# The expert gather of a two-model program: 12 row buffers for U in three quads, 12 for V in three rotating sets, V groups up to five behind U groups, and head queries one chunk earlier

## What is computed

```python
def peer_ffn(xm, w_query, sub_keys, expert_u, expert_v):      # per layer
    q = (xblk @ w_query).reshape(B, 128, 8, 2, 256)            # 8 heads, 512 wide
    s = einsum('bthpd,hpnd->bthpn', q, sub_keys)               # 2 x 128 key scores a head
    vals, idx = lax.top_k(s, 16)
    cand = vals[..., 0, :, None] + vals[..., 1, None, :]       # 256 candidates
    top_s, pos = lax.top_k(cand, 16)
    eidx = take_along_axis(cand_idx, pos)                      # 16 of 16384 experts
    g = softmax(top_s)
    h = einsum('btd,bthkd->bthk', xblk, expert_u[eidx])        # 16 dot products
    act = gelu(h) * g
    return einsum('bthk,bthkd->btd', act, expert_v[eidx])      # sum of 16 rows
```

## Time and profile before

| | |
|---|---|
| median of 3 runs | 3297.96 us (3285.51 to 3304.04) |
| profiled execution, span from first to last instruction | 3263.7 us, 34.3 us less than the median |
| instructions | 34887 |
| gather of layer 0 / layer 1 | about 240 to 1018 us / 1225 to 2005 us |
| busy: PE, DVE, ACT, POOL | 75%, 64%, 29%, 32% of the span |
| DMA | 886.31 MB; 536.94 MB of them by POOL's indirect DMAs |

### The profile page before, as it was taken

The page is one execution under the profiler, slowest core; times in us unless marked ns, Lnnn a source line. Parts: engine busy times, 40 slices in busy tenths (PEclk is TensorE's granted clock), DMA queues, the critical chain, the costliest instruction groups (busy, mean ns, idle before and its releaser), DMA issues.

```text
span 3263.7 us, 34887 instructions
## 1 busy us (share of the span) xinstructions
PE 2431.9 (75%) x12607; PEld 1727.6 (53%) x12607; DVE 2088.5 (64%) x4416; ACT 933.8 (29%) x1486; POOL 1043.1 (32%) x1060
## 2 busy tenths in 40 slices
PE   5996555544546997555545545999999999999998
PEld 4754422221103764422221102789879988997797
DVE  7878576666656958576666654655555555556654
ACT  3511011110112421011101112544554446445543
POOL 0105566666663105566566663100010001000000
PEclk9998777766667998677666766989999999999999
DMA  9858999999999839999999998345534542554353
GB/s 363 299 209 332 353 374 380 378 379 365 361 378 341 295 139 342 350 370 394 377 359 372 356 365 307 131 143 191 180 130 155 180 168 82 190 194 155 110 193 123
DMA packets 308642, 886.31 MB, mean 272 GB/s; under 512 B 22824, under 2 KB 32144, under 8 KB 308240
## 3 DMA queue, kind: packets, MB, share of 16 engines
q0 software_dynamic: 147456, 536.94, 42.9%
q1 hardware_dynamic: 161040, 347.51, 29.9%
HBM read 883.32 MB, written 1.05 MB: 271 GB/s over the span
## 4 chain that ended last, share of the span: by engine, by line
PE 46%; issue 31%; DVE 9%; another core or an unknown queue 6%; DMA 4%; SPq 2%; ACT 2%; POOL 1%; DVEq 0%; ACTq 0%; POOLq 0%
PE lin L837 7%; PE lin L838 7%; PE lin L839 7%; PE psT L839 2%; PE psT L838 2%; PE psS L838 2%; PE psS L839 2%; PE psT L837 2%; PE psS L837 2%; PE lin L1141 2%; PE psS L1097 2%; PE psS L887 2%; DMA ring<-in_w_in 2%; PE lin L1014 1%
## 5 line engine op out<-in xcount | busy, mean ns | idle before, releaser
L2454 DVE CUSTOM_DVE_ANT_0 proj<-proj,psT 128x1024 f32<-128x1024 f32 x512 | 606.1, 1218 | 211.1 <-DMA proj<-in_expert_u,eidx 120.5
L1928 DVE TENSOR_TENSOR weights_split<-ring,weights_split 128x1024 fp32r<-128x1024 f32 (+1 forms) x360 | 431.5, 1207 | 376.2 <-ACT weights_split L1712 373.6
L2787 POOL DMA_INDIRECT proj<-in_expert_u,eidx x512 | 481.5, 940 | 424.7 <-DVEq L2430 212.7
L1712 ACT ACTIVATE weights_split<-ring 128x1024 fp32r<-128x1024 f32 (+1 forms) x376 | 391.5, 1046 | 467.7 <-PE lin L839 291.6
L1141 PE MATMUL lin<-vbuf,rowb 128*32 128x512 f32 x1024 | 252.0, 879 | 266.8 <-issue 180.4
L2823 POOL TENSOR_TENSOR weights_split<-ring,weights_split 128x1024 fp32r<-128x1024 f32 x16 | 37.9, 2376 | 995.3 <-ACT weights_split L1712 995.3
L1141 PE MATMUL lin<-ring,rowb 128*32 128x512 f32 x896 | 208.8, 755 | 153.1 <-issue 107.1
L837 PE MATMUL lin<-weights_split,xT_high 128*128 128x512 f32 (+1 forms) x736 | 295.0, 401 | 19.6 <-issue 8.2
L839 PE MATMUL lin<-weights_split,xT_high 128*128 128x512 f32 (+1 forms) x736 | 288.1, 391 | 0.0
L2800 POOL DMA_INDIRECT ring<-in_expert_v,pT x224 | 211.0, 942 | 231.4 <-remote 86.8
L2800 POOL DMA_INDIRECT vbuf<-in_expert_v,pT x256 | 241.2, 942 | 115.5 <-issue 76.5
(11 more groups left out here) (336 smaller groups left out, 4943.9 us busy)
## 6 DMA issues: line engine op xcount, KB each, us to landing
ring<-in_mlp_w_up SPq DMA_DIRECT2D x32, 2048.0 KB, 8.1
ring<-in_mlp_w_down SPq DMA_DIRECT2D x32, 2048.0 KB, 7.9
ring<-in_w_in SPq DMA_DIRECT2D x14, 2048.0 KB, 14.1
ring<-in_w_query SPq DMA_DIRECT2D x14, 2048.0 KB
vbuf<-in_ada_w SPq DMA_DIRECT2D x12, 2048.0 KB, 12.9
ring<-in_diff_w_in SPq DMA_DIRECT2D x11, 2048.0 KB, 8.1
proj<-in_ada_w SPq DMA_DIRECT2D x24, 512.0 KB, 5.1
ring<-in_moba_w_in SPq DMA_DIRECT2D x6, 2048.0 KB, 8.0
```

Source lines behind the costliest of these rows:

```text
L1712: act.activation(part(p, 0, kind, w), raw_piece(slot, p, kind, w), ACT.Copy).then_inc(hi_ready, 1)
L1928: dve.tensor_tensor(part(p, 1, kind, w), raw_piece(slot, p, kind, w), part(p, 0, kind, w).bitcast(F32), ALU.subtract).then_inc(lo_ready, 1)
L2454: dve.tensor_tensor_reduce(ubuf[:, n % GB, :], ubuf[:, n % GB, :], x_row, 1.0, 0.0, ALU.mult, ALU.add, hdot[:, cb, k:k + 1]).then_inc(h_re ...
L2787: pool.indirect_dma_start(out=ubuf[:, (16 * c + k) % GB, :], out_offset=None, in_=table["u"], in_offset=bass.IndirectOffsetOnAxis(ap=eidx[ ...
```

## The change

U gets twelve rows in three quads: the old eight and `ring3`. `UQUAD` gives each group its quad: 0, 1, 0, 1 for the first four, then 2, 0, 1 in turn; a group waits for the dots of the last group that used its quad. Quad 2 is granted by `u_free` at the place of the second credit of L1249. V keeps three sets of buffers, used in rotation by the running number of the group and not by the set within the chunk; the last V group of a layer (63) goes to the quad of U group 61. The first credits of `v_free` are three in place of four, so V group 2 waits for the credit of L1258 and V group 3 for the sum of set 0. `LAGS` puts V groups behind U groups by 2, 2, 3, 4 in chunks 0 to 3, by 5 in chunks 4 to 13, and by 4 and 3 in the last two. `indices_by_pair(c + 2)` moves ahead of all sets of chunk c. Heads 4 to 7 are asked in chunks 3, 5, 7, 9 in place of 4, 6, 8, 10, with half the query behind the second set and half, with the key scores, behind the third (chunks 1 and 2: behind the first and the second, as before), and the keys' transposes no longer ahead of the chunk's sets. DVE's waits on `v_free` are renumbered to mean the same sums.

```diff
@@ -50,9 +50,13 @@
 NSET = 4
 SETROWS = TOPK // NSET
-VLAG = 2
-LANDED = 16 * PH * NT * TOPK // GB
-VLANDED = 16 * SETROWS * PH * NT
+NVB = 3
+GROUPS = 4 * PH * NT
+UQUAD = [0, 1, 0, 1] + [(2, 0, 1)[i % 3] for i in range(GROUPS - 4)]
+UBEFORE = [max([j for j in range(i) if UQUAD[j] == UQUAD[i]], default=None) for i in range(GROUPS)]
+UTIMES = [UQUAD[:i + 1].count(UQUAD[i]) for i in range(GROUPS)]
+VBUF = [q % NVB for q in range(GROUPS - 1)] + [NVB]
+VTIMES = [VBUF.count(b) for b in range(NVB + 1)]
 DEPTH2 = 4
@@ -204,7 +208,8 @@
 NCH = len(CHUNKS)
 ROWS_TAKEN = [1 + sum(CHUNKS[i][1] != CHUNKS[i - 1][1] for i in range(1, c + 1)) for c in range(NCH)]
-ASKED = {1: 2, 2: 3, 4: 4, 6: 5, 8: 6, 10: 7}
+ASKED = {1: 2, 2: 3, 3: 4, 5: 5, 7: 6, 9: 7}
+LAGS = [2, 2, 3, 4] + [5] * (NCH - 6) + [4, 3]
 SUM_AT = {u: q for q, u in enumerate(SUMS)}
@@ -346,15 +351,21 @@
             return {8: psS[:, 1, :], 0: psT[:, 0, :], 2: psT[:, 1, :], 4: lin[:, 2, :], 6: lin[:, 3, :]}[b]
 
-        def vrow(i):
-
-            if i < 4:
-                return vbuf[:, i, :]
-            if i < 8:
-                return ring3[:, (i - 4) * D:(i - 3) * D]
-            if i < 12:
-                return ring2[:, (i - 8) * D:(i - 7) * D] if i < 11 else pr1
-            return vbuf[:, i - 8, :]
+        def urow(i, b):
+
+            if UQUAD[i] == 2:
+                return ring3[:, b * D:(b + 1) * D]
+            return ubuf[:, 4 * UQUAD[i] + b, :]
+
+        def vrow(q, b):
+
+            if VBUF[q] == NVB:
+                return urow(GROUPS - 3, b)
+            if VBUF[q] == 0:
+                return vbuf[:, b, :]
+            if VBUF[q] == 1:
+                return ring2[:, b * D:(b + 1) * D] if b < 3 else pr1
+            return vbuf[:, 4 + b, :]
 
@@ -486,8 +497,8 @@
         ps_used = sem("peer_scores_copied")
         idx_ready = sem("expert_indices_ready")
-        u_ld = [sem(f"u_rows_landed{i}") for i in range(GB)]
-        v_ld = [sem(f"v_set_landed{i}") for i in range(NSET)]
+        u_ld = [sem(f"u_rows_landed{i}") for i in range(GB + SETROWS)]
+        v_ld = [sem(f"v_set_landed{i}") for i in range(NVB + 1)]
         u_free = sem("u_buffer_free")
@@ -690,7 +701,7 @@
                         sp.wait_ge(sk_done, h - 1)
                     keys_load(h)
-                sp.wait_ge(v_free, NSET * 2 * PH)
+                sp.wait_ge(v_free, NVB + GROUPS - NSET)
                 sp.wait_ge(xr_ready, ROWS_TAKEN[-1])
@@ -700,8 +711,8 @@
                 if l + 1 < DEPTH:
                     params(l + 1)
-                for s in range(NSET):
-                    sp.wait_ge(v_ld[s], (l + 1) * VLANDED)
+                for b in range(NVB + 1):
+                    sp.wait_ge(v_ld[b], (l + 1) * 64 * VTIMES[b])
                 first_unit(T["w_in"][l + 1] if l + 1 < DEPTH else T["diff_w_in_2"][0])
@@ -1130,27 +1141,30 @@
                     last = c >= NCH - NT
                     pe.wait_ge(wst_ready, c + 1)
+                    if 0 < c < NCH - 2:
+                        indices_by_pair(c + 2)
                     for s in range(NSET):
-                        if s == 2 and 0 < c < NCH - 2:
-                            indices_by_pair(c + 2)
                         if c == NCH - 1 and s == NSET - 1:
                             pe.sem_inc(arrive, 1)
-                        pe.wait_ge(v_ld[s], l * VLANDED + 64 * (c + 1))
+                        q = NSET * c + s
+                        pe.wait_ge(v_ld[VBUF[q]], 64 * (l * VTIMES[VBUF[q]] + VBUF[:q + 1].count(VBUF[q])))
                         for half in range(2):
                             for b in range(4):
                                 mm = pe.matmul(lin[32 * b:32 * b + 32, 2 * half + t, :], wst[:, c % 2, 4 * b + s, :],
-                                               vrow(SETROWS * s + b)[:, half * 512:(half + 1) * 512], start=False, stop=last and s == NSET - 1,
+                                               vrow(q, b)[:, half * 512:(half + 1) * 512], start=False, stop=last and s == NSET - 1,
                                                skip_group_check=True)
...
                         elif s == NSET - 1:
                             mm.then_inc(last_sum, 1)
-                        if c in ASKED and s < 2:
-                            if c == 1 and s == 0:
+                        if c in ASKED:
+                            if s == (0 if c < 3 else 1):
                                 query_keys(ASKED[c])
-                            query_rows(ASKED[c], 2 * s)
-                            query_rows(ASKED[c], 2 * s + 1)
-                            if s == 1:
+                                query_rows(ASKED[c], 0)
+                                query_rows(ASKED[c], 1)
+                            if s == (1 if c < 3 else 2):
+                                query_rows(ASKED[c], 2)
+                                query_rows(ASKED[c], 3)
                                 key_scores(ASKED[c])
@@ -1246,7 +1260,8 @@
                 half_linear(3, 1, xT, KC, out_columns(1))
                 pe.wait_ge(lin_done, lin0 + 12)
-                pe.sem_inc(v_free, 2)
+                pe.sem_inc(v_free, 1)
+                pe.sem_inc(u_free, 4)
                 normed_rows(1, lambda g: lin[:, g, :])
@@ -1271,8 +1286,6 @@
                 for c in range(1, NCH):
                     weights_by_pair(c)
-                    if c in ASKED and c > 1:
-                        query_keys(ASKED[c])
                     expert_sum(c)
@@ -2412,7 +2425,7 @@
                         link(dve.tensor_tensor(m(0), down(vals[:, 0, :]), along(vals[:, 1, :]), ALU.add))
                         if c >= 4:
-                            dve.wait_ge(v_free, 4 * c - 8)
+                            dve.wait_ge(v_free, NVB + 4 * (c - 3))
                         top16(sc2[:, 4, :], sc2[:, 5, :], 256, tops[:, cb, :], posu[:, 0, :])
@@ -2449,9 +2462,10 @@
                     dve.wait_ge(xr_ready, ROWS_TAKEN[c])
                     for k in range(TOPK):
-                        n = 16 * c + k
-                        dve.wait_ge(u_ld[n % GB], l * LANDED + (32 * c + 16 * (k // GB + 1)))
-                        dve.tensor_tensor_reduce(ubuf[:, n % GB, :], ubuf[:, n % GB, :], x_row, 1.0, 0.0,
+                        i, b = 4 * c + k // 4, k % 4
+                        times = l * UQUAD.count(UQUAD[i]) + UTIMES[i]
+                        dve.wait_ge(u_ld[4 * UQUAD[i] + b], 16 * times)
+                        dve.tensor_tensor_reduce(urow(i, b), urow(i, b), x_row, 1.0, 0.0,
                                                  ALU.mult, ALU.add, hdot[:, cb, k:k + 1]).then_inc(h_ready, 1)
@@ -2473,7 +2487,7 @@
 
                     if c >= 2:
-                        dve.wait_ge(v_free, 4 * c)
+                        dve.wait_ge(v_free, NVB + 4 * (c - 1))
                     dve.wait_ge(wt_done, c + 1)
@@ -2545,7 +2559,7 @@
                 for t in range(NT):
                     if t == 0:
-                        dve.wait_ge(v_free, NSET * 2 * PH)
+                        dve.wait_ge(v_free, NVB + GROUPS - NSET)
                     else:
@@ -2776,38 +2790,43 @@
                 def u_rows(c, g):
 
-                    n = 16 * c + 4 * g
+                    i = 4 * c + g
                     if g == 0:
                         pool.wait_ge(idx_ready, c + 1)
-                    if n >= GB:
-                        pool.wait_ge(h_ready, n - GB + 4)
+                    if UBEFORE[i] is not None:
+                        pool.wait_ge(h_ready, 4 * UBEFORE[i] + 4)
                     else:
-                        pool.wait_ge(u_free, n + 4)
-                    for k in range(4 * g, 4 * g + 4):
+                        pool.wait_ge(u_free, 4 * (UQUAD[i] + 1))
+                    for b in range(4):
                         pool.indirect_dma_start(
-                            out=ubuf[:, (16 * c + k) % GB, :], out_offset=None, in_=table["u"],
-                            in_offset=bass.IndirectOffsetOnAxis(ap=eidx[:, c % 4, k:k + 1], axis=0),
-                        ).then_inc(u_ld[(16 * c + k) % GB], 16)
+                            out=urow(i, b), out_offset=None, in_=table["u"],
+                            in_offset=bass.IndirectOffsetOnAxis(ap=eidx[:, c % 4, 4 * g + b:4 * g + b + 1], axis=0),
+                        ).then_inc(u_ld[4 * UQUAD[i] + b], 16)
 
...
                     if s == 0:
                         pool.wait_ge(it_used, c + 1)
-                    pool.wait_ge(v_free, q + 1)
+                    if q < GROUPS - 1:
+                        pool.wait_ge(v_free, q + 1)
+                    else:
+                        pool.wait_ge(h_ready, 4 * (GROUPS - 2))
                     for b in range(SETROWS):
                         g = 4 * b + s
                         pool.indirect_dma_start(
-                            out=vrow(SETROWS * s + b), out_offset=None, in_=table["v"],
+                            out=vrow(q, b), out_offset=None, in_=table["v"],
```

(14 more changed lines are left out.)

## The result

The changed kernel took 3492.14 us (median of 4 runs, 3485.54 to 3500.24) against 3299.82 for the kernel before (4 runs): a ratio of 1.0588, 95% interval 1.0561 to 1.0616. It is 192 us slower; 3272 was forecast, and the range ended at 3348.

What follows compares the result with a forecast made beforehand. DMA was taken as near its ceiling, with winnable hollows where V groups wait for PE to free sets. 54 less 12 less 15 gives 27, less 14 at the start 13 a layer, 26 in all: 3272 us, range 3222 to 3348.

Steps and rivals of the forecast that it cites:

- The likeliest case: The forecast itself: V's waits shrink in mid layer; 26 us faster in all, 3272 us (3250 to 3290), chance 0.37.
- The rival "slower": DVE's wait for weights behind set 4c-1: PE over 5 us late in most chunks, POOL stops; 3348 us, chance 0.30.
- Step "The price of that": Mid layer: DVE now hangs on PE's sum of set 4c-1, slack 5 us; 12 us a layer, bounds 0, 40.
- The start: Start of each layer: edits delay U group 10 by 26 us; 14 us lost a layer, bounds -3 and 32.
- Steps 1 and 2: Layer start: V group 2 waits for a later credit, V group 3 for its sum; U group 6 21 us later.
- Step 4: Layer start: chunk 3's indices, ahead of chunk 1's first sum, hold V group 7; U group 10 26 us late.
- I take 12: Recovery of the start's loss by U group 20: 12 us, where DMA's ceiling allowed 14.5.
- The bounds after it, -3 and 32: Bounds of the start's net loss a layer, taken as 14 us: a gain of 3 to a loss of 32.
- Mid layer's 54 us: Mid layer and tail: hollows of 46 and 8 us a layer, where DMA runs below 410 GB/s, winnable.
- The sum's base: Span of the profiled execution, 3263.7 us, 34.3 below the median; what lies around it taken as unchanged.
- The ceiling: DMA in gather: 410 GB/s held for 29 us taken as attainable, against the skill page's 358, by which time would be 3326.
- the full case: PE keeps its pace whatever DMA does and asked chunks fit: 40 us a layer gained, 3218 us, chance 0.08.

Runs made afterwards that it cites:

- e3: Changed kernel with V groups three behind U groups from chunk 2 on: 3342.05 us, ratio 1.0143.
- e6: Changed kernel with four chained one-column memsets on POOL ahead of each group of indirect DMAs: 3428.17 us, ratio 1.0427.
- e12: Changed kernel with four memsets ahead of each group, and ACT's copy of the query's second half moved behind the next chunk's gelu: 3412.12 us, ratio 1.0374.
- e2: Changed kernel with the indices of chunk 3 back between the second and third set of chunk 1: 3455.97 us, ratio 1.0487.
- e8: Changed kernel with V three groups behind, chunk 3's indices back between chunk 1's sets, next chunk's weights ahead of the last set: 3301.61 us, ratio 1.0038.
- e14: Changed kernel with V three groups behind, chunk 3's indices back between chunk 1's sets, query halves one set earlier, no memsets: 3314.98 us, ratio 1.0066.
- e17: Changed kernel, lag 5 kept, chunk 3's indices back between chunk 1's sets, query halves one set earlier, five memsets a group: 3273.66 us, ratio 0.9971.
- e15: Kernel before with five memsets on POOL ahead of each group of indirect DMAs: 3260.05 us, ratio 0.9911.
- e1: Changed kernel with the weights of chunk c+1 made ahead of the last set of chunk c, from c = 3 on: 3465.58 us, ratio 1.0515.
- e4: Kernel before with one memset on POOL ahead of each group of four indirect DMAs: 3302.24 us, ratio 1.003.
- e7: Changed kernel with V groups four behind U groups in mid layer, three in chunk 2: 3364.06 us, ratio 1.0241.
- e13: Changed kernel, lag 5 kept, chunk 3's indices back between chunk 1's sets, query halves one set earlier, no memsets: 3353.31 us, ratio 1.0183.
- n = 7: Kernel before with seven memsets on POOL ahead of each group of indirect DMAs: 3275.57 us, ratio 0.9947.
- n = 0: Kernel before with no memsets added: ratio 1.

## Why the prediction was wrong, point by point

**The sign.** The likeliest case fell. The rival "slower" named the place, DVE's wait for weights behind set 4c-1, and its condition, that PE is over 5 us late there in most chunks. It held. Its price of 20 us of waits a layer was wrong: in mid layer they were 123, and even this rival's 3348 is 144 us short.

**Step "The price of that": the term that failed.** It counted landing, sum and stationaries at their durations, found 5 us of slack, and let only a half query break it, by 3 us in four chunks, 12 us a layer and 40 at most. The U line waited 123.3 us in mid layer 1 and mid layer grew by 69 and 73 us, all of which goes with lag 3 (e3). Two things were left out. In the changed kernel the post of PE's weights reached DVE 13 to 16 us after PE's record wherever DVE waited for it in mid layer; that took the whole slack (waits of 11 us where there is no query, all but the last gone in e6). And ACT was not followed: the gelu of chunk c+1 stands in its queue behind the query's copies, so a later query holds DVE by way of ACT (30.89 us in e6). The half query ahead of the fourth set itself was sized about rightly: 6.49 us in one wait of e12 where 7 to 8 were worked out. The nearest sign in the kernel before was PE's slow records: I read the one at 1655.63 and the query of the earlier trace rows as PE's pace, charged it against V's slack, and didn't apply it to the new and shorter slack of DVE. That they and the late posts are one thing isn't shown; the kernel before has no late post of weights.

**The start.** Steps 1 and 2 came out: V group 2 waited 15.0 us for the credit and V group 3 11.1 for its sum. Step 4 came out in kind, 32.1 us instead of some 22. U group 10 was 40 us late in layer 1 (161 against 121) and 45 in layer 0, where 26 was taken and 37 the bound. "I take 12" of recovery was more or less there (11 and 18 us to U20), but mostly as the shift of V groups into the tail, so it wasn't a gain. The bounds after it, -3 and 32, don't follow from 3, 37 and 12, which give -9 and 25. e2 shows the index order as 33 us of the whole. Credits and the third set may be what is left: 12 us in e8 and 22 in e14 over the kernel before, 20 in e17 over e15. That is inferred and wasn't tried alone.

**Mid layer's 54 us.** The V waits did fall as forecast (82.6 to 25.1 us). That they are worth time was the error: 1 - 370/410 took 410 GB/s, reached for 29 us, as what DMA could hold on the mean. In 20 traces no mid layer ran faster than 462 us from U20 to U60, and no window of a whole mid layer read above 374 GB/s, with waits of 76 us or of none. Here most of POOL's waits are where DMA's backlog is worked off, not hollows. The share of 0.97 in the earlier trace rows said so, and I read past it.

**The sum's base.** I took the 34.3 us between the profiled span and the median as lying around the span. By the later results a span is 2 us below its run's time, so the profiled execution of the kernel before was itself 1% shorter than the median. One place of it is visible: V group 1 of layer 0 waited 2.85 us there, and 20 to 22 in the traces of e1, e3, e4, e7, e8, e13 and e14.

**The ceiling and the full case.** A stretch of 29 us can hold 410 GB/s, but the mid layers of the kernels that come near the one before read 366 to 374 as a whole, and 358 with n = 7. The Trainium skill's page "DMA: Bandwidth & Descriptors", Bandwidth, gave about 358 GB/s as what binds transfers from HBM, and I set it aside for the row of 410. The runs lie between: the means are nearer to the page's figure than to my ceiling, but it doesn't bind as stated, since the stretch and nearly all the means lie above it. The Trainium skill's page "SBUF — State Buffer", section "SBUF: two separate sides", says that no compute operation slows a DMA or the reverse. No run here shows two ports in contention. But PE did not keep its pace: its 48 unexplained gaps at n = 0 fell to 3 at n = 7. So the case I built on that page was wrong.

## What to carry to other kernels

Before moving work behind a transfer, list for every engine what then stands in its queue behind that wait, ACT's copies included, and hold the slack left against the longest gap between a producer's record and the engine that waits for it, not against the durations. A wait of the issuing engine is worth time only if the DMA engines are idle in it; read the busy share over the whole stage ahead of the peak rate of a good stretch. If the issuer outruns DMA, try slowing it a little: three to seven memsets gave the kernel before 0.3 to 0.9%, though three cost one form of the change 0.4%.

## What was not expected of the hardware

In stretches of full DMA, semaphores seem to reach the waiting engine long after the record of the instruction that posts them (PE to DVE 15.1 us, PE to ACT 20.5 us in e12 and 25.2 without memsets), while instructions of PE and DVE can follow one another slowly (PE's records of the earlier trace rows at 2.8 us; three of DVE at 1694.68, 1696.07 and 1697.47 us in the changed kernel, 1.4 apart). In the changed kernel without memsets the wait at U group 27 ends as the queues run empty. The slow records fade as POOL issues slower. The late posts don't simply: memsets took them from the weights of most chunks of the changed kernel (e6), but with three to five of them late posts appeared in the kernel before, which had none without; with seven they were gone again. So fullness has a part in it, e6 says, but isn't enough by itself, and by which path it acts is open. The second is that a busy share of 0.97 stood beside 358 as well as 373 GB/s, so the share alone doesn't say how near to its best rate DMA is.
